# Attention on one Trainium2 core: MLA heads' p times v in two passes, with denominators summed in PSUM, remainders on GpSimd, and v split by ScalarE and GpSimd

## What is computed

```python
def _attend_queries(q, k, v, scale):
    s = jnp.einsum('bqhgd,bkhd->bhgqk', q, k, preferred_element_type=jnp.float32) * scale
    p = jax.nn.softmax(s, axis=-1).astype(v.dtype)
    return jnp.einsum('bhgqk,bkhe->bqhge', p, v)
```

## Time and profile before

| | |
|---|---|
| median of 3 runs | 4045.94 us (4045.75 to 4050.45) |
| the profiled execution | 4051.12 us, its span 4049.3 us |
| TensorE busy | 3724.0 us, 92% |
| VectorE busy | 2759.5 us, 68% |
| ScalarE busy | 2378.7 us, 59% |
| GpSimd busy | 558.6 us, 14% |
| mean granted TensorE clock | 0.957 |

### The profile page before, as it was taken

How to read it: one execution, slowest core, us unless ns; L and a number is a source line. 1 busy time by engine, 2 the same in 40 slices (tenths; PEclk the granted TensorE clock), 3 DMA queues, 4 the chain that set the end, 5 groups by cost and what they waited for, 6 DMA issues and landing times. The chain is left out here.

```text
span 4049.3 us, 53075 instructions
## 1 busy us (share of the span) xinstructions
PE 3724.0 (92%) x16747; PEld 2721.7 (67%) x16748; DVE 2759.5 (68%) x4431; ACT 2378.7 (59%) x4129; POOL 558.6 (14%) x553
## 2 busy tenths in 40 slices
PE   7999948999999999999999999998999479999992
PEld 7888825666666666677767677766888446666661
DVE  5666547888888898878777777854444556666564
ACT  4343303777777777766766767677333045555554
POOL 0000000111111111111110111100000023343330
PEclk9999967999999999999999999999999789999996
DMA  4464662221222212220221122002343068888877
GB/s 168 152 215 161 205 171 78 62 43 25 62 62 62 44 32 54 62 60 7 62 61 41 26 62 50 17 7 70 140 145 125 33 205 240 255 242 235 238 229 275
DMA packets 307899, 453.81 MB, mean 112 GB/s; under 512 B 118198, under 2 KB 245458, under 8 KB 296818
## 3 DMA queue, kind: packets, MB, share of 16 engines
q1 hardware_dynamic: 241766, 359.65, 30.0%
q0 software_dynamic: 18576, 67.64, 7.2%
q10 hardware_dynamic: 47376, 24.26, 2.1%
HBM read 305.48 MB, written 145.85 MB: 111 GB/s over the span
## 5 line engine op out<-in xcount | busy, mean ns | idle before, releaser
L941 ACT ACTIVATE b_p_hi<-b_psS 128x512 fp32r<-128x512 f32 (+1 forms) x1376 | 822.2, 598 | 540.0 <-PE b_psS L1072 531.0
L1072 PE MATMUL b_psS<-b_q,b_k 96*128 96x512 f32 (+3 forms) x3440 | 1047.2, 402 | 4.9 <-DMA b_q<-b_nmxT 2.7
L989 DVE TENSOR_TENSOR b_p_lo<-b_prob,b_p_hi 128x512 fp32r<-128x512 f32 x1152 | 824.9, 717 | 245.0 <-ACT b_prob L944 219.0
L944 ACT ACTIVATE b_prob<-b_psS 128x512 f32<-128x512 f32 (+1 forms) x1376 | 815.2, 592 | 1.1
L1072 PEld LDWEIGHTS b_psS<-b_q,b_k 96*128 96x128 f32 (+3 forms) x3440 | 627.1, 185 | 233.4 <-ACT b_prob L944 7.9
L997 DVE TENSOR_REDUCE b_mx_s<-b_psM 128x1 f32<-128x512 f32 x1024 | 690.1, 686 | 76.3 <-PE b_psM L1103 63.6
L1103 PE MATMUL b_psM<-b_k,b_q 128*128 128x512 f32 (+1 forms) x1280 | 511.7, 421 | 49.6 <-DMA b_v<-V 39.5
L1095 PE MATMUL b_psO<-b_p_hi,b_v_hi 128*65 128x512 f32 x1280 | 514.2, 402 | 16.7 <-DVE b_p_lo L989 15.2
L1095 PE MATMUL b_psO<-b_p_lo,b_v_hi 128*65 128x512 f32 x1280 | 507.6, 397 | 0.0
L1095 PE MATMUL b_psO<-b_p_hi,b_v_lo 128*65 128x512 f32 x1280 | 507.4, 396 | 0.0
L930 POOL TENSOR_TENSOR b_p_lo<-b_prob,b_p_hi 128x512 fp32r<-128x512 f32 x128 | 165.2, 1290 | 1662.4 <-ACT b_prob L944 1662.4
(11 more groups left out here) (247 smaller groups left out, 5228.4 us busy)
## 6 DMA issues: line engine op xcount, KB each, us to landing
e_w_gu<-w_gate SPq DMA_DIRECT2D x32, 1024.0 KB, 7.6
e_w_gu<-w_up SPq DMA_DIRECT2D x32, 1024.0 KB, 9.8
e_w_dn<-w_down SPq DMA_DIRECT2D x32, 1024.0 KB, 13.5
a_x_raw<-xallT SPq DMA_DIRECT2D x25, 512.0 KB, 4.9
a_x<-xall SPq DMA_DIRECT2D x25, 512.0 KB, 4.2
c_o<-O SPq DMA_DIRECT2D x24, 512.0 KB, 4.9
c_x<-xall SPq DMA_DIRECT2D x24, 512.0 KB, 3.3
H<-c_h SPq DMA_DIRECT2D x24, 512.0 KB, 2.6
```

The source lines that it names most:

```text
L941: nc.scalar.activation(p_hi[0:kn, (s * NI + j) % NP, :], psS[0:kn, j % 2, :], ACT.Exp)
L944: nc.scalar.activation(prob[0:kn, (s * NI + j) % NP, :], psS[0:kn, j % 2, :], ACT.Exp).then_inc(p_ready, 1)
L989: nc.vector.tensor_tensor(out, prob[0:kn, slot, :], p_hi[0:kn, slot, :].bitcast(F32), ALU.subtract).then_inc(lo_ready, 1)
L1072: m = nc.tensor.matmul(psS[0:kn, j % 2, :], kk[s][0:r, k], qq[s][0:r, q], start=n == 0, stop=n == len(passes) - 1)
```

## The change

MLA heads: v's remainder and rounded half lie side by side as 128 weight columns, so p_hi x (v_lo | v_hi) is one pass and p_lo x (v_lo | v_hi) another; 128 rows of `psO` are copied, and the block end adds the two halves with a matmul against `pair_id` (two identities on top of each other). The denominator has no column any more: VectorE adds the full p, item by item, into a PSUM bank (`acc`), the last item's sum goes to SBUF (`accS`), and TensorE multiplies it with ones. The remainder of p is made by GpSimd for all MLA items; in GQA heads VectorE and GpSimd share it as before.

p times v is issued in two parts in all heads: `pv_hi` two items behind `qk`, `pv_lo` four. p has five slots. The meta item is the second of its block; in GQA heads it takes two passes. v is loaded without ones into one buffer `v_raw`; ScalarE makes the rounded half and GpSimd the remainder, in three pieces of eight chunks, both between items. Units go only to items at which VectorE neither normalises nor has a meta item; a second unit of the same item stands between `pv_hi` and `pv_lo`. The meta maxima use a bank of `psM`, whose place the sum takes. The core of the diff:

```diff
+        v = [sb(f"v_{s}", [P, TILES, 2 * VD + 1], F32R) for s in range(2)]
+        v_raw = sb("v_raw", [P, TILES + 1, VD])
+        REST, HIGH, ROUNDED, BOTH = slice(0, VD), slice(VD, 2 * VD), slice(VD, 2 * VD + 1), slice(0, 2 * VD)
-        NP = 4
+        NP = 5
+        acc = ps("acc", [P, W])
-        R = 4
-        SPAN = 72
+        R = 6
+        HI_LAG, LO_LAG, SPLIT_LAG, DEN_LAG = 2, 4, 2, 3
+        SPAN = 70
+        calm = [j for j in range(R, R + SPAN) if j - 7 not in END_OF and ITEMS[j - DEN_LAG][2] != META]
         for u in range(NU):
-            UNIT_AT.setdefault(R + u * SPAN // NU, []).append(u)
+            UNIT_AT.setdefault(calm[u * len(calm) // NU], []).append(u)
+        V_AT = {16: slice(8, 16), 22: slice(16, 24), 40: slice(0, 8)}
...
         @block.sync  # load()
+                if h > 0:
+                    sp.wait_ge(v_ready, 2 * h - (1 if part == "s" else 0))
+                    sp.sem_inc(carrier, 1)
...
         @block.gpsimd
+            def remainder(h, s, gqa, j):
+                if META_ITEM[j] or not on_pool(gqa, j):
+                    return
+                slot = slot_of(h, j)
+                pool.wait_ge(p_ready, h * NI + j + 3)
+                nc.gpsimd.tensor_tensor(p_lo[:, slot, :], prob[:, slot, :], p_hi[:, slot, :].bitcast(F32),
+                                        ALU.subtract).then_inc(lo_ready, 1)
...
+                for j in range(NI):
+                    remainder(h, s, gqa, j)
+                    if not last and j in V_AT:
+                        v_rest(h + 1, V_AT[j])
...
         @block.scalar
+                if not gqa:
+                    act.wait_ge(den_done, (h - GH) * NI + j + 1)
+                slot = slot_of(h, j)
+                nc.scalar.activation(p_hi[0:kn, slot, :], psS[0:kn, j % 2, :], ACT.Exp)
+                nc.scalar.activation(prob[0:kn, slot, :], psS[0:kn, j % 2, :], ACT.Exp).then_inc(p_ready, 1)
...
+                nc.scalar.activation(v[s][:, c, HIGH], v_raw[:, c, :], ACT.Copy).then_inc(v_rounded, 1)
...
+                    if not last and j + 3 in V_AT:
+                        v_round(h + 1, i + s, nxt, V_AT[j + 3])
...
         @block.vector
+            def meta_rest(h, s, j):
+                slot = slot_of(h, j)
+                nc.vector.tensor_tensor(p_hi[M_LO, slot, :], prob[M_HI, slot, :], p_hi[M_HI, slot, :].bitcast(F32),
+                                        ALU.subtract).then_inc(meta_lo_ready, 1)
...
+            def den_add(h, s, j):
+                _, _, kn, _, first, last = ITEMS[j]
+                slot = slot_of(h, j)
+                dve.wait_ge(p_ready, h * NI + j + 3)
+                if META_ITEM[j]:
+                    meta_rest(h, s, j)
+                dve.wait_ge(den_done, (h - GH) * NI + j + NP)
+                if first:
+                    m = nc.vector.tensor_copy(acc[:, :], prob[:, slot, :])
+                else:
+                    out = accS[:, :] if last else acc[0:kn, :]
+                    m = nc.vector.tensor_tensor(out, acc[0:kn, :], prob[0:kn, slot, :], ALU.add)
+                m.then_inc(den_done, 1)
...
+            dve.wait_ge(ident_loaded, 16)
+            nc.vector.tensor_tensor(pair_id[:, :], ident[:, 0:VD], ident[:, VD:2 * VD], ALU.add)
             nc.vector.memset(p_hi[:, :, :].bitcast(F32), 0.0)
...
         @block.tensor
+            def pv_hi(h, s, gqa, j):
...
+                p = p_hi[:, slot_of(h, j), :]
+                if gqa:
+                    nc.tensor.matmul(psO[0:VD + 1, b % 2, :], v[s][:, vc, ROUNDED], p, start=first, stop=False)
+                    nc.tensor.matmul(psO[0:VD, b % 2, :], v[s][:, vc, REST], p, start=False, stop=False)
+                else:
+                    nc.tensor.matmul(psO[:, b % 2, :], v[s][:, vc, BOTH], p, start=first, stop=False)
...
+            def pv_lo(h, s, gqa, j):
...
+                ready, n = rest_of(h, j, gqa)
+                pe.wait_ge(ready, n)
+                r, cols = (VD + 1, ROUNDED) if gqa else (P, BOTH)
+                nc.tensor.matmul(psO[0:r, b % 2, :], v[s][:, vc, cols], p_lo[:, slot_of(h, j), :],
+                                 start=False, stop=last).then_inc(pv_done, 1)
...
+            def o_turn(h, b, u, gqa):
...
+                        nc.tensor.matmul(psT[:, c * VD:c * VD + VD], oT[:, b % 2, cc], pair_id[:, :], start=True, stop=True)
+                        m = nc.tensor.matmul(psT[:, SUP * VD + c:SUP * VD + c + 1], accS[:, cc], ones[:, :],
+                                             start=True, stop=True)
```

More of the change, by code:

```diff
@@ new lines, in stage_attend, with on_pool, rest_of @@
+        FINISH_AT, ROW_AT = R + SPAN, R + SPAN + 3
+        POOL_EVERY = 8
+        V_AT = {16: slice(8, 16), 22: slice(16, 24), 40: slice(0, 8)}
+        META_ITEM = [kn == META for _, _, kn, _, _, _ in ITEMS]
+        NKEY = META_ITEM.count(False)
+        ON_POOL = [j for j in range(24, NI - 3) if j % POOL_EVERY == 0 and not META_ITEM[j]]
+        POOL_GQA, DVE_GQA = len(ON_POOL), NKEY - len(ON_POOL)
+        def on_pool(gqa, j):
+            return not gqa or j in ON_POOL
+        def rest_of(h, j, gqa):
+            n = META_ITEM[:j].count(False) + 1
+            if not gqa:
+                return lo_ready, GH * POOL_GQA + (h - GH) * NKEY + n
+            before = sum(k < j for k in ON_POOL)
+            if j in ON_POOL:
+                return lo_ready, h * POOL_GQA + before + 1
+            return lo_ready_dve, h * DVE_GQA + n - before
@@ L795, in o_store @@
         def o_store(engine, h, b):
-            engine.wait_ge(o_ready, h * NB + b + 1)
+            engine.wait_ge(o_ready, h * NB + b + 3)
             if engine is not nc.scalar:
@@ new lines, in remainder, with v_rest @@
+            def remainder(h, s, gqa, j):
[5 more added lines that the diff above has]
+                                        ALU.subtract).then_inc(lo_ready, 1)
+            def v_rest(n, c):
+                s = n % 2
+                if c.start == SEQ // P:
+                    pool.wait_ge(v_rounded, 3 * n + 1)
+                elif c.start > 0:
+                    pool.wait_ge(v_rounded, 3 * n + 2)
+                else:
+                    pool.wait_ge(v_rounded, 3 * n + 3)
+                m = nc.gpsimd.tensor_tensor(v[s][:, c, REST], v_raw[:, c, :], v[s][:, c, HIGH].bitcast(F32), ALU.subtract)
+                if c.start == 0:
+                    for rows in (M_HI, M_LO):
+                        pool.drain()
+                        m = nc.gpsimd.tensor_tensor(v_meta[s][rows, REST], v_raw[M_HI, TILES, :],
+                                                    v_meta[s][M_HI, HIGH].bitcast(F32), ALU.subtract)
+                    pool.drain()
+                if c.stop == TILES or c.start == 0:
@@ L1039, in _ @@
             row(0, 0)
-            for j in range(R - 1):
-                remainder(0, 0, j)
+            dve.sem_inc(den_done, NP)
+            for j in range(R - SPLIT_LAG):
+                split(0, 0, j)
             def head(h, i, s, gqa, nxt, last):
                 for j in range(R, NI):
-                    remainder(h, s, j - 1)
+                    follow(h, s, gqa, j - lag(gqa))
                     if not last:
@@ L1087, in pv @@
                 if first:
                     pe.wait_ge(ot_ready, h * NB + b + 1)
-                slot = (s * NI + j) % NP
-                if ITEMS[j][2] == META:
-                    nc.tensor.matmul(psO[0:VC, b % 2, :], v_meta[s][:, :], p_hi[:, slot, :],
-                                     start=first, stop=last).then_inc(pv_done, 1)
-                    return
-                for n, (vv, pp) in enumerate(((v_hi, p_hi), (v_lo, p_hi), (v_hi, p_lo))):
-                    m = nc.tensor.matmul(psO[0:VC, b % 2, :], vv[s][:, vc, :], pp[:, slot, :],
-                                         start=first and n == 0, stop=last and n == 2)
@@ L1139, in _, with unit_of @@
                 qk(0, 0, True, j)
-                if j >= 2:
-                    pv(0, 0, j - 2, 0)
+                if j >= HI_LAG:
+                    pv_hi(0, 0, True, j - HI_LAG)
+                if j >= LO_LAG:
+                    pv_lo(0, 0, True, j - LO_LAG)
+            def unit_of(h, i1, s, nxt, u):
+                if u == 0:
+                    pe.wait_ge(ld_s[1 - s], loads_seen(i1, nxt, "s"))
+                if UNITS[u][0] == 0 and UNITS[u][2] == 0:
+                    pe.wait_ge(ld_p[1 - s], loads_seen(i1, nxt, "p"))
+                unit(h + 1, 1 - s, nxt, u)
             def head(h, i, s, gqa, nxt, last):
-                block_of = [sum(e < j for e, _ in BLOCKS_END) for j in range(NI)]
                 i1 = i + s
```

297 lines of the change are left out of this document (165 added, 132 removed).

## The result

The kernel after takes 4071.97 us (median of 4 runs, 4070.46 to 4077.58) against 4047.14 (4045.75 to 4050.45) beside it: ratio 1.0063 [1.0045, 1.0080]. It is slower by 25 us where 3930 was predicted, so 142 us have to be found.

What follows compares the result with a forecast made beforehand. TensorE was taken as the bound everywhere, VectorE close behind in GQA heads. 8 x -13.5 (MLA) - 8 x 1.8 (GQA) + 3.2 (start) + 1 (end) = -118 us, from 4051.1 to 3933, 3928 against the median; predicted 3930, range 3900 to 3990.

Steps and rivals of the forecast that it cites:

- Passes: MLA p times v on TensorE: two passes instead of three, 80 fewer per head at 0.232, -18.6 us.
- Block ends: MLA block ends on TensorE: four transposes become eight small matmuls, 0.90 us against 0.24, +4.0 us per head.
- The upper bound of twice the price: MLA block ends: small matmuls at twice 0.112 us, should their weight loads cost more, +9.3 us per head.
- The stated condition: Prediction is wrong if a block-end small matmul costs far from 0.11 us, or either engine's pitch is off over 0.1.
- Meta items: p times v of meta items: GQA two passes instead of one, +1.4 us per head; MLA still one.
- The engines: MLA heads: VectorE 117.5 us, GpSimd 109 to 119, under TensorE's 125.0; rivals VectorE bound (3970, 0.20), GpSimd's pace (3955, 0.11).
- lock: Rival: GpSimd's remainders lock out VectorE's additions in MLA heads, +21 us per head, about 4205; chance 0.07.
- the upper bound of 0.72: VectorE's additions in MLA heads: 0.72 us instead of 0.60 to 0.61 if each waits for the one before.
- the kind that was called contended: VectorE operations with both inputs in SBUF, slowed beside GpSimd: two took 3.08 us instead of 1.3.
- Stalls 4.5: TensorE standing still per MLA head: 4.5 us, 3.4 before; VectorE's meta or normalising places may hold units back.
- Start +3.2: Kernel start: VectorE waits for ident and clears five slots instead of four, +3.2 us, between 1 and 4.
- it does not do what it says: Rival: MLA 128-column passes at 0.29 us and block ends at twice the price pay back the saving, 4040; chance 0.04.

Runs made afterwards that it cites:

- e4: Kernel before, with six more plain float32 matmuls (12 on TensorE) ahead of each MLA block end, into unread columns: 4109.26 us, ratio 1.0161.
- e2: Changed kernel, with the meta items' p times v passes over all 128 rows instead of 16 and 48: 3980.10 us, ratio 0.9835.
- e14: Changed kernel, with meta passes over 65 rows instead of 16 and 48: 3981.99 us, ratio 0.9844.
- e3: Changed kernel, MLA block ends as four 65-row transposes, without adding halves or the denominator's product (MLA output not the reference's): 3958.36 us, ratio 0.9790.
- e6: Changed kernel, with the MLA block end's small matmuls kept together but issued, with the normalising, one item later: 4014.18 us, ratio 0.9913.
- e11: Changed kernel, remainder half issued first at MLA block ends, so one 128-row pass stands between 48-row pass and small matmuls: 4052.25 us, ratio 1.0021.
- e8: e2, but in MLA heads VectorE adds only each block's first, meta and last item and GpSimd makes no remainders: 3967.16 us, ratio 0.9805.

## Why the prediction failed

- *Passes, -18.6 us per MLA head: right.* 504 passes at 0.232 with 128 columns of weights; the row sum above has nothing else in that place.
- *Block ends, "eight small matmuls ... 8 x 0.112 = 0.90": wrong by a factor of two.* The price of one held (0.12; 0.11 in e4), the count didn't: plain float32 is two matmuls each, 16 x 0.12 = 1.9. It is +5.5 us per MLA head, 44 us in all. The upper bound of twice the price (+9.3 over the old transposes, 9.5 measured) all but covered it, by luck: it was set for dearer weight loads, and nothing in the text looked at the types of the operands. The stated condition ("a small matmul at a block end costs far from 0.11 us") was met per instruction: 0.24.
- *Meta items, "MLA: still one", GQA "+6 x 0.232": mis-sized.* I costed a pass over 16 or 48 rows at the pitch of 128 rows; the meta passes of before read 128 rows, so no row showed the other. In GQA heads it is the miss: with full rows (e2) the head has the forecast 123.5, with 48 and 16 rows 126.4, of which 1.8 us are steps and 1.1 more clock excess.
- *The clock: not a term at all.* The earlier trace rows has it granted in full nearly everywhere, and I carried that over to a different mix of work; no rival names it either. It is 11.0 us per MLA head in the four heads and 78 us in all eight, where the trace before has 9. Of the time at the lower level in the four heads, the three quarters behind block ends are new. e2 and e14 show that the height of the meta pass is a condition for them, e3 that the row of small matmuls is another; e6 and e11 show that they get fewer when the two are moved apart, with part of the wait for `oT` gone in both. Why these conditions lower the clock stays open.
- *The engines: right, with one price off.* Additions at 0.692 us a record, no lock, no wait of TensorE for GpSimd or VectorE in the four heads; e8 gives 1.6 us per head for both. With a maximum between them an addition costs the forecast 0.60 us, but two additions one behind the other start 0.78 to 0.81 us apart in the trace after (107 pairs), more than the upper bound of 0.72. That didn't matter, as TensorE had the later end. Only the six meta remainders per head, the kind that was called contended, are slower beside GpSimd: 0.98 us where they had 0.68.
- *Stalls 4.5: right in size (4.1) by luck.* The forecast put them on VectorE's thin lead; 2.5 of them lie at the meta passes, in the steps of their height and the waits for `oT` behind them, and 1.0 is spread over q times k.
- *Start +3.2: +6.0* between the two traces' first rows of maxima.

The sum with the two terms put right is 129.5 + 5.5 + 11.0 = 146.0, what the trace has. With the block ends put right and the clock quiet, the forecast's own arithmetic gives 129.5 + 5.5 = 135.0; e2 measures 136.5 and e14 133.7. The rival "it does not do what it says" (4040) had the block ends at twice the price, which came true, and dearer 128-column passes, which didn't. The change's idea was worth 1.6% and not 2.9%, and its slices of 16 and 48 rows turned it into a loss.

## What to carry to other kernels

- Before pricing a matmul, look at the type of both operands, and hold the count in the trace against the instructions in the kernel: here the plain float32 ones stand there twice. The small ones here went from 1.3 to 10.9 us per head and took back half of the 18.6 that the saved passes gave.
- A saved row of zeros saves nothing on TensorE: slicing the contraction to 48 or 16 rows between 128-row passes cost 0.1 to 0.15 us per change, and close ahead of 16 small matmuls it cost the clock. Keep one height through a stream, or try it.
- A sum at full clock is a forecast for a stream like the one that was traced. Where a change puts short, small or low matmuls close together, read the clock by windows of a few us first; a busy share near 100% hides it.

## What the runs showed of the hardware

- The granted clock falls to the lower level and stays there while TensorE has no gap (6.80 of 6.80 us busy at 0.53), with no wait ahead of it over 0.8 us in four heads. The Trainium skill (TensorE: Matmul & The Clock Gate, section HAM oscillation — how this bites in real kernels) explains such falls by long waits of TensorE for DMA; no such wait is in these heads.
- us per MLA head at the lower level, by meta pass and small matmuls per block end, in brackets the part behind block ends: 48 rows and 16: 25.6 (18.8); 128 and 16: 6.8 (3.4); 65 and 16: 0.9 (0); 48 and 4: 5.1 (0); 128 and 4: 4.3 (0). The rest lies at the row of 24 small matmuls of the meta maxima, 3.4 in the kernel before.
- Additions from PSUM and SBUF into PSUM take 0.692 us on VectorE for 128x512, with GpSimd busy 74% of the time beside them; GpSimd's own record rises from 1.29 to 1.33.
